# The third low half of the sums ahead of the second unit's slab, in a float32 encoder layer

## The chip, the cores and the metric

The kernel runs on one core of one Trainium2 chip. The metric is the time of one execution on the device in microseconds, the median of several runs; less is better. The core has five engines with instruction queues of their own, which run in order: TensorE (PE, matmuls), VectorE (DVE), ScalarE (ACT), GpSimd (POOL) and SyncE (SP), which here only issues DMAs. They are tied together by semaphores.

## The reference

One layer of a streaming encoder over 512 tokens of width 1024, all in float32:

```python
x = x + 0.5 * swiglu(rms_norm(x, ffn1_norm), ffn1_gate, ffn1_up, ffn1_down)
x = x + hybrid_mixer(rms_norm(x, mix_norm), ...)
x = x + 0.5 * swiglu(rms_norm(x, ffn2_norm), ffn2_gate, ffn2_up, ffn2_down)
return rms_norm(x, final_norm)

def swiglu(h, w_gate, w_up, w_down):
    return (jax.nn.silu(h @ w_gate) * (h @ w_up)) @ w_down
```

The hidden width of a feed-forward is 2816, which is 22 tiles of 128. The mixer (gated linear attention, differential attention and a short convolution) isn't touched here.

## The kernel before

Every float32 product is made as three matmuls of rounded operands: an operand a is split into a high half (a copy to float32r, made by ScalarE) and a low half (a minus its high half, made by VectorE), and `three` (lines 570 to 574) multiplies high by high, high by low and low by high. So each slab of weights, once loaded into `raw`, passes through ScalarE's `split_hi` (line 1118, tile `w_hi`) and VectorE's `split_lo` (line 1496, tile `w_lo`) before TensorE can use it. A slab is 128 partitions by 1024 elements.

A feed-forward has 22 hidden tiles. The first four (`pair`) multiply a gate slab and an up slab in the plain way. The other 18 are **units** of a Strassen-like scheme with seven half-size products in place of eight. A unit v loads a gate slab into `raw` and an up slab into `raw_u`, both double-buffered by v modulo 2. GpSimd (`sums`, lines 483 to 503) makes four sums of their halves:

- T1 = a half of the gate slab plus a half of the up slab (line 491). It waits for both loads, and for VectorE to have read the T1 of the unit before (`ga_lo`).
- T3 = the two halves of the up slab (line 495); T2 = T1 plus the other half of the up slab (line 498); T4 = T2 plus the other half of the gate slab, written over the first half of `raw_u` (line 502). T4 waits for the gate slab's low half (`lo_ready`).

GpSimd makes them in the order T1, T3, T2, T4. ScalarE makes three high halves of them and VectorE three low halves: `ga` (T1 and T2, lines 1198 and 1558), `gb` (T3, lines 1205 and 1563) and `gc` (T4 with the other half of `raw_u`, lines 1237 and 1568).

TensorE's seven products of a unit are M1 and M2 (from the gate slab), M6 and M5 (from ga), M7 (from gb), M4 and M3 (from gc). Its order over units is M1 M2 of unit v, M4 M3 of unit v-1, M6 M5 M7 of unit v; for unit 0 there is no M4 M3 in between. Three products of a unit add up in the same PSUM bank, and ScalarE copies its intermediate states out (`take`, line 1213, tile `snap`): after M1, after M6 and after M7. VectorE combines them: `c11` (lines 1616 and 1619), `c12` (1588), `c21` (1582), `c22` (1576), and `gated` (1596) multiplies with the SiLU that ScalarE makes (1219).

The order of the engines is written out by hand. In VectorE's `unit(v)`: c22 of the unit before, ga, gb, the split of the next unit's slab, c21 of the unit before, c11, c12 of the unit before, gc, gated of the unit before. In ScalarE's: the snapshot of M7 of the unit before, gb, the high half of the next slab, the snapshot of M1, SiLU of the unit before, gc, the snapshot of M6, and ga of the next unit. For unit 0, which has no unit before it, ga and gb are made in the last `pair`, and VectorE's `unit` has only the split of unit 1's slab, c11 and gc.

SyncE's loads (`load_unit`, line 388 on) come in one queue: for unit v the gate slab once T4 of unit v-2 is done (line 396), then the up slab once `gc_lo` of unit v-2 has been counted (line 401). In the first feed-forward alone, a bias table for the mixer is made between units 1 and 2: two matmuls on TensorE (line 590) and two operations on VectorE that follow `gated` of unit 0.

Of the kernel before, what the change touches and what calls it, by code (L numbers as in the profile page):

```python
# [176 lines left out]
def build_layer(nc, xT, up_w, down_w, t_w, dv_w, nat_w, out_w, gains, gk_up, gk_bias, gla_gain, diff_gain,  # L177
                lam_qk, rel_bias, conv_w, onehot, decay_mats, level_masks, ident_c, out):
    tvec = nc.dram_tensor("bias_by_distance", (HEADS * COPIES, 5 * P), F32, kind="Internal")
    with ExitStack() as ctx:  # L180
# [1296 lines left out]
        def _(dve):  # L1477
# [8 lines left out]
            def split_lo(s, n=0):  # L1486

                if isinstance(s, int) and s >= END:
                    return
                dve.wait_ge(hi_ready, n + (s + 1))  # L1490
                w = slab_width(s)
                lo, hi = w_lo[:, slot(s), 0:w], w_hi[:, slot(s), 0:w]
                if isinstance(s, int) and isinstance(n, int) and s >= END - 3:
                    k = KT * (s - (END - 3))
                    lo, hi = (t[:, k:k + w // P, :].rearrange("p k c -> p (k c)") for t in (last_lo, last_hi))
                dve.tensor_tensor(lo, raw[:, slot(s), 0:w], hi, ALU.subtract).then_inc(lo_ready, 1)  # L1496
# [26 lines left out]
            def ffn_up(f, up0):  # L1523
# [32 lines left out]
                def ga(i, b):  # L1556
                    dve.wait_ge(ga_hi, 2 * i + b + (FAST * f + 1))
                    dve.tensor_tensor(sum_lo[:, GA, :], t_raw[:, GA, :], sum_hi[:, GA, :], ALU.subtract)\
                        .then_inc(ga_lo, 1)

                def gb(i, b):
                    dve.wait_ge(gb_hi, 2 * i + b + (FAST * f + 1))
                    dve.tensor_tensor(sum_lo[:, GB, :], t_raw[:, GB, :], sum_hi[:, GB, :], ALU.subtract)\
                        .then_inc(gb_lo, 1)

                def gc(i, b):
                    dve.wait_ge(gc_hi, 2 * i + b + (FAST * f + 1))
                    dve.tensor_tensor(sum_lo[:, GC, :], raw_u[:, b, :].rearrange("p (a c) -> p a c", a=2),
                                      sum_hi[:, GC, :], ALU.subtract).then_inc(gc_lo, 1)

                def c22(i, b):

                    v = 2 * i + b
                    dve.wait_ge(snap_ready[2], v + (FAST * f + 1))
                    dve.wait_ge(m5_done, v + (FAST * f + 1))
                    dve.scalar_tensor_tensor(h[:, PLAIN + v, HALF:S], ps[:, B_BANK[b], 0:HALF], -1.0, snap[:, 2, :],
                                             ALU.mult, ALU.subtract).then_inc(c22_done, 1)

                def c21(i, b):
                    v = 2 * i + b  # L1580
                    dve.wait_ge(m4_done, v + (FAST * f + 1))
                    dve.tensor_tensor(gate_s[:, b, HALF:S], ps[:, A_BANK[b], 0:HALF], rinv[:, HALF:S], ALU.mult)\  # L1582
                        .then_inc(c21_scaled, 1)

                def c12(i, b):
                    v = 2 * i + b
                    dve.wait_ge(m3_done, v + (FAST * f + 1))
                    dve.scalar_tensor_tensor(h[:, PLAIN + v, 0:HALF], ps[:, B_BANK[b], 0:HALF], -1.0, snap[:, 1, :],
                                             ALU.mult, ALU.subtract).then_inc(c12_done, 1)

                def gated(i, b):
                    v = 2 * i + b
                    dve.wait_ge(c12_done, v + (FAST * f + 1))
                    dve.wait_ge(c22_done, v + (FAST * f + 1))
                    dve.wait_ge(silu_done, v + (FT * f + PLAIN + 1))
                    dve.tensor_tensor(h[:, PLAIN + v, :], h[:, PLAIN + v, :], gate_s[:, b, :], ALU.mult)\
                        .then_inc(h_ready, 1)

                def unit(i, b, prev, following):

                    v = 2 * i + b
                    s = up0 + 2 * PLAIN + b
                    if prev:
                        c22(*prev)
                        ga(i, b)
                        gb(i, b)
                    if following:
                        split_lo(s + 1, 2 * i)
                    else:
                        split_lo(s + 2 * i + 1)  # L1610
                    if prev:
                        c21(*prev)
                    dve.wait_ge(h_ready, v + (FT * f + PLAIN - 1))
                    dve.wait_ge(snap_ready[0], v + (FAST * f + 1))
                    dve.wait_ge(slab_used, 2 * i + (s + 1))
                    dve.tensor_tensor(gate_s[:, b, 0:HALF], ps[:, C_BANK[b], 0:HALF], snap[:, 0, :], ALU.add)\
                        .then_inc(c11_added, 1)
                    dve.wait_ge(c11_added, v + (FAST * f + 1))
                    dve.tensor_tensor(gate_s[:, b, 0:HALF], gate_s[:, b, 0:HALF], rinv[:, 0:HALF], ALU.mult)\
                        .then_inc(c11_scaled, 1)  # L1620
                    if prev:
                        c12(*prev)
                    gc(i, b)
                    if prev:
                        gated(*prev)

                for m in range(PLAIN):
                    pair(m)
                unit(0, 0, None, (0, 1))
                unit(0, 1, (0, 0), (1, 0))  # L1630
                if f == 0:
                    bias_table()
                with dve.Fori(1, FAST // 2 - 1) as i:
                    unit(i, 0, (i - 1, 1), (i, 1))
                    unit(i, 1, (i, 0), (i + 1, 0))
# [536 lines left out]
```

## Time and profile before

| | before |
|---|---|
| median of 3 runs | 953.16 us (952.85 to 953.86) |
| profiled execution | 953.2 us, span 951.4 us |
| TensorE matmul busy | 941.7 us (99%) |
| VectorE busy | 685.9 us (72%) |
| ScalarE busy | 435.9 us (46%) |
| GpSimd busy | 358.2 us (38%) |
| granted TensorE clock | 1.00 |

The span runs from the first to the last instruction of the core; the time of the execution holds a little more. Busy is the time in which an engine had an instruction running; one that stands still inside an instruction counts as busy.

### The profile page before, as it was taken

How to read it: one execution, taken by the hardware profiler on the slowest of the kernel's cores; microseconds unless marked ns; L12 is line 12 of the kernel's file. 1: busy time of each engine (PE TensorE's matmuls, PEld its weight loads, DVE VectorE, ACT ScalarE, POOL GpSimd, SP SyncE). 2: the span in 40 equal slices, each digit the busy share in tenths (PEclk: the TensorE clock that was granted, in tenths of full speed). 3: DMA queues.
4: the chain of work that ended last, by engine and by line, in shares of the span. 5: the costliest groups of instructions: out<-in, count | busy, mean ns of one | idle time of the engine just before them, and what ended most of it. 6: DMA issues, size and time to landing. Idle time of an engine off the chain costs nothing.

```text
span 951.4 us, 16549 instructions
## 1 busy us (share of the span) xinstructions
PE 941.7 (99%) x6290; PEld 843.0 (89%) x6290; DVE 685.9 (72%) x956; ACT 435.9 (46%) x686; POOL 358.2 (38%) x241
## 2 busy tenths in 40 slices
PE   9999999999999999999999999999999999999997
PEld 7899999999888889777899788889999999988887
DVE  6699999998543375677578964379999999833444
ACT  7565454556522233654534323544555555632331
POOL 0777777762010135110100015387767676000001
PEclk9999999999999999999999999999999999999999
DMA  6323333232222325222212123233242322232322
GB/s 211 117 105 109 112 95 125 88 131 71 90 100 100 104 79 170 75 74 78 72 57 68 46 88 106 71 133 112 89 132 88 125 96 98 80 100 77 102 99 89
DMA packets 31104, 94.27 MB, mean 99 GB/s; under 512 B 4464, under 2 KB 7712, under 8 KB 31056
## 3 DMA queue, kind: packets, MB, share of 16 engines
q1 hardware_dynamic: 29120, 90.28, 28.8%
q0 software_dynamic: 1648, 3.07, 1.3%
q8 instruction: 33, 0.54, 0.2%
q10 hardware_dynamic: 288, 0.26, 0.1%
q14 instruction: 15, 0.12, 0.0%
HBM read 90.38 MB, written 2.42 MB: 98 GB/s over the span
## 4 chain that ended last, share of the span: by engine, by line
PE 86%; DVE 6%; POOL 2%; ACT 2%; issue 1%; DMA 1%; SPq 0%; DVEq 0%; ACTq 0%; POOLq 0%
PE ps L572 27%; PE ps L574 26%; PE ps L573 26%; POOL h L516 2%; DVE w_lo L1496 1%; DVE s_lo L1553 1%; PE ps L851 1%; PE ps L931 1%; PE ps L872 1%; PE ps L904 1%; ACT h L1126 1%; DVE states L1883 1%; ACT w_hi L1118 1%; DMA x<-xT 0%; PE ps L861 0%
## 5 line engine op out<-in xcount | busy, mean ns | idle before, releaser
L1496 DVE TENSOR_TENSOR w_lo<-raw,w_hi 128x1024 fp32r<-128x1024 f32 (+2 forms) x128 | 195.9, 1530 | 146.0 <-ACT w_hi L1118 146.0
L1118 ACT ACTIVATE w_hi<-raw 128x1024 fp32r<-128x1024 f32 (+2 forms) x128 | 131.3, 1026 | 193.1 <-PE ps L574 193.1
L572 PE MATMUL ps<-xg_hi,w_hi 128*128 128x256 f32 (+1 forms) x528 | 178.2, 338 | 0.8 <-DVE w_lo L1496 0.6
L574 PE MATMUL ps<-xg_hi,w_lo 128*128 128x256 f32 (+1 forms) x528 | 175.0, 331 | 0.0
L573 PE MATMUL ps<-xg_lo,w_hi 128*128 128x256 f32 (+1 forms) x528 | 174.8, 331 | 0.0
L572 PE MATMUL ps<-s_hi,sum_hi 128*128 128x256 f32 x576 | 160.1, 278 | 1.2 <-ACT snap L1213 0.9
L573 PE MATMUL ps<-s_lo,sum_hi 128*128 128x256 f32 x576 | 159.4, 277 | 0.0
L574 PE MATMUL ps<-s_hi,sum_lo 128*128 128x256 f32 x576 | 159.2, 276 | 0.0
L573 PE MATMUL ps<-h_lo,w_hi 128*128 128x512 f32 x330 | 128.4, 389 | 0.0
L572 PEld LDWEIGHTS ps<-xg_hi,w_hi 128*128 128x128 f32 x528 | 99.9, 189 | 19.1 <-issue 8.2
L572 PEld LDWEIGHTS ps<-s_hi,sum_hi 128*128 128x128 f32 x576 | 108.3, 188 | 2.0 <-issue 1.7
L574 PEld LDWEIGHTS ps<-xg_hi,w_lo 128*128 128x128 f32 x528 | 99.9, 189 | 9.9
L573 PEld LDWEIGHTS ps<-s_lo,sum_hi 128*128 128x128 f32 x576 | 108.3, 188 | 0.0
L574 PEld LDWEIGHTS ps<-s_hi,sum_lo 128*128 128x128 f32 x576 | 108.2, 188 | 0.0
L573 PEld LDWEIGHTS ps<-xg_lo,w_hi 128*128 128x128 f32 x528 | 99.9, 189 | 8.5
L574 PE MATMUL ps<-h_hi_s,w_lo 128*128 128x512 f32 x240 | 93.4, 389 | 0.0
L572 PE MATMUL ps<-h_hi_s,w_hi 128*128 128x512 f32 x240 | 93.4, 389 | 0.0
L491 POOL TENSOR_TENSOR t_raw<-raw,raw_u 128x512 f32<-128x512 f32 x36 | 54.9, 1526 | 79.5 <-DMA raw_u<-up_w 68.5
L495 POOL TENSOR_TENSOR t_raw<-raw_u 128x512 f32<-128x512 f32 x36 | 79.6, 2212 | 0.0
L502 POOL TENSOR_TENSOR raw_u<-t_raw,raw 128x512 f32<-128x512 f32 x36 | 71.9, 1998 | 11.5 <-POOL t_raw L498 7.0
L573 PEld LDWEIGHTS ps<-h_lo,w_hi 128*128 128x128 f32 x330 | 62.0, 188 | 12.6
L1219 ACT ACTIVATE gate_s<-gate_s 128x512 f32<-128x512 f32 x34 | 21.5, 634 | 110.5 <-DVE gate_s L1582 110.5
(255 smaller groups left out, 1891.5 us busy)
## 6 DMA issues: line engine op xcount, KB each, us to landing
raw<-up_w SPq DMA_DIRECT2D x50, 512.0 KB, 4.1
raw<-down_w SPq DMA_DIRECT2D x38, 512.0 KB, 3.2
raw_u<-up_w SPq DMA_DIRECT2D x36, 512.0 KB, 3.2
raw<-t_w SPq DMA_DIRECT2D x15, 512.0 KB, 3.2
raw<-out_w SPq DMA_DIRECT2D x8, 512.0 KB, 3.2
raw<-nat_w SPq DMA_DIRECT2D x4, 576.0 KB, 3.8
x<-xT SPq DMA_DIRECT2D x8, 256.0 KB, 4.8
out<-x SPq DMA_DIRECT2D x8, 256.0 KB, 2.2
```

The costliest lines, as they stand in the source:

```text
L491: pool.tensor_tensor(t_raw[:, T1, :], raw[:, slot(s), 0:HW], raw_u[:, b, 0:HW], ALU.add)\
L495: pool.tensor_tensor(t_raw[:, T3, :], raw_u[:, b, 0:HW], raw_u[:, b, HW:UPW], ALU.add)\
L502: pool.tensor_tensor(raw_u[:, b, 0:HW], t_raw[:, T2, :], raw[:, slot(s), HW:UPW], ALU.add)\
L516: pool.tensor_tensor(out_ap, in0, in1, op).then_inc(s_made, 1)
L572: pe.matmul(out_ap, a[0], b[0], start=first, stop=False, skip_group_check=resumed)
L573: pe.matmul(out_ap, a[0], b[1], start=False, stop=False, skip_group_check=resumed)
L574: return pe.matmul(out_ap, a[1], b[0], start=False, stop=last, skip_group_check=resumed)
L851: last = pe.matmul(ps[:, 4 + mp, 0:w], dqk[r, h % 2, 0, i * P:(i + 1) * P], dqk[r, h % 2, 1, 0:w], start=True, stop=True)
L872: last = pe.matmul(ps[:, 7, 0:DV], pT[:, n % 2, b * P:(b + 1) * P], dv[:, b, h * DV:(h + 1) * DV], start=b == 0, stop=b == i)
L1118: act.activation(dst, raw[:, slot(s), 0:w], ACT.Copy).then_inc(hi_ready, 1)
L1219: act.activation(gate_s[:, b, :], gate_s[:, b, :], ACT.Silu).then_inc(silu_done, 1)
L1496: dve.tensor_tensor(lo, raw[:, slot(s), 0:w], hi, ALU.subtract).then_inc(lo_ready, 1)
```

## The change

In `unit` of VectorE's feed-forward, for the first unit (the one without a `prev`), `gc` is issued ahead of `split_lo` of the next unit's slab; before, it was issued last, behind c11. All other units keep their order. The code is used by both feed-forwards, so two places of the run are touched.

```diff
@@ -1604,6 +1604,8 @@
                         c22(*prev)
                         ga(i, b)
                         gb(i, b)
+                    else:
+                        gc(i, b)
                     if following:
                         split_lo(s + 1, 2 * i)
                     else:
@@ -1620,8 +1622,7 @@
                         .then_inc(c11_scaled, 1)
                     if prev:
                         c12(*prev)
-                    gc(i, b)
-                    if prev:
+                        gc(i, b)
                         gated(*prev)
```

## Rows read from the trace of the kernel before

**Rows 1.** The page: busy us, share of the span and instructions of each engine.

```profile
PE 941.7 (99%) x6290; PEld 843.0 (89%) x6290; DVE 685.9 (72%) x956; ACT 435.9 (46%) x686; POOL 358.2 (38%) x241
```

**Rows 2.** Timeline of TensorE, second feed-forward: start us, length us, instruction, idle before and releaser.

```profile
648.99 0.28 PE L572 MATMUL ps<-xg_hi,w_hi 128*128 128x256 f32 x1
...
657.62 0.36 PE L572 MATMUL ps<-s_hi,sum_hi 128*128 128x256 f32 x1
...
667.36 0.28 PE L574 MATMUL ps<-s_hi,sum_lo 128*128 128x256 f32 x1
668.50 0.36 PE L572 MATMUL ps<-s_hi,sum_hi 128*128 128x256 f32 x1 [0.86 <-ACT snap L1213]
```

**Rows 3.** Chain that ended last, from 640 to 672 us: start us, us, what.

```profile
651.39 3.20 DMA raw_u<-up_w
```

**Rows 4.** Timeline of VectorE, second feed-forward, units 0 to 2.

```profile
642.39 2.33 DVE L1558 TENSOR_TENSOR sum_lo<-t_raw,sum_hi 128x1024 fp32r<-128x1024 f32 x1
...
645.84 1.72 DVE L1496 TENSOR_TENSOR w_lo<-raw,w_hi 128x1024 fp32r<-128x1024 f32 x1
...
648.91 2.31 DVE L1568 TENSOR_TENSOR sum_lo<-raw_u,sum_hi 128x1024 fp32r<-128x1024 f32 x1
651.54 0.42 DVE L1576 SCALAR_TENSOR_TENSOR h<-ps,snap 128x256 f32<-128x256 f32 x1 [0.32 <-ACT snap L1213]
651.88 1.58 DVE L1558 TENSOR_TENSOR sum_lo<-t_raw,sum_hi 128x1024 fp32r<-128x1024 f32 x1
...
653.98 1.21 DVE L1496 TENSOR_TENSOR w_lo<-raw,w_hi 128x1024 fp32r<-128x1024 f32 x1
...
658.79 1.78 DVE L1596 TENSOR_TENSOR h<-h,gate_s 128x512 f32<-128x512 f32 x1
661.55 0.42 DVE L1576 SCALAR_TENSOR_TENSOR h<-ps,snap 128x256 f32 x1 [0.99 <-ACT snap L1213]
...
663.77 2.31 DVE L1496 TENSOR_TENSOR w_lo<-raw,w_hi 128x1024 fp32r<-128x1024 f32 x1
```

**Rows 5.** Timeline of GpSimd, second feed-forward, units 1 to 3.

```profile
644.89 1.59 POOL L491 TENSOR_TENSOR t_raw<-raw,raw_u 128x512 f32<-128x512 f32 x1 [1.25 <-DVE sum_lo L1558]
646.43 2.27 POOL L495 TENSOR_TENSOR t_raw<-raw_u 128x512 f32<-128x512 f32 x1
648.66 1.48 POOL L498 TENSOR_TENSOR t_raw<-t_raw,raw_u 128x512 f32<-128x512 f32 x1
...
654.75 1.60 POOL L491 TENSOR_TENSOR t_raw<-raw,raw_u 128x512 f32<-128x512 f32 x1 [2.38 <-DMA raw_u<-up_w]
...
663.42 1.57 POOL L491 TENSOR_TENSOR t_raw<-raw,raw_u 128x512 f32<-128x512 f32 x1 [1.70 <-DVE sum_lo L1558]
```

**Rows 6.** Timeline of ScalarE, second feed-forward: three snapshots.

```profile
651.15 0.36 ACT L1213 ACTIVATE snap<-ps 128x256 f32<-128x256 f32 x1
...
657.12 0.36 ACT L1213 ACTIVATE snap<-ps 128x256 f32<-128x256 f32 x1
...
667.99 0.36 ACT L1213 ACTIVATE snap<-ps 128x256 f32<-128x256 f32 x1
```

**Rows 7.** Timeline of VectorE, first feed-forward: the splits for units 1 and 2.

```profile
58.76 1.71 DVE L1496 TENSOR_TENSOR w_lo<-raw,w_hi 128x1024 fp32r<-128x1024 f32 x1
...
66.91 1.21 DVE L1496 TENSOR_TENSOR w_lo<-raw,w_hi 128x1024 fp32r<-128x1024 f32 x1
```

**Rows 8.** Timeline of GpSimd, first feed-forward: T1 and T2 of unit 1.

```profile
57.81 1.59 POOL L491 TENSOR_TENSOR t_raw<-raw,raw_u 128x512 f32<-128x512 f32 x1 [1.25 <-DVE sum_lo L1558]
...
61.59 1.48 POOL L498 TENSOR_TENSOR t_raw<-t_raw,raw_u 128x512 f32<-128x512 f32 x1
```

**Rows 9.** Timeline of ScalarE, first feed-forward: the snapshot of M6 of unit 1.

```profile
70.03 0.36 ACT L1213 ACTIVATE snap<-ps 128x256 f32<-128x256 f32 x1
```

**Rows 10.** Timeline of TensorE, first feed-forward: M1 and M7 of unit 1.

```profile
62.05 0.28 PE L572 MATMUL ps<-xg_hi,w_hi 128*128 128x256 f32 x1
...
70.54 0.36 PE L572 MATMUL ps<-s_hi,sum_hi 128*128 128x256 f32 x1
```

## The prediction

> **What bounds the kernel.** I read the page first: TensorE is busy 941.7 us of a span of 951.4 [rows 1]. It sets the time nearly everywhere, so an edit on VectorE counts only where TensorE waits. The second view is TensorE's timeline in the first units of a feed-forward [rows 2]. Below, M1 to M7 are a unit's seven products. TensorE makes M1 and M2 of a unit from its slab, then M4 and M3 of the unit before, then M6, M5 and M7 of the unit itself. T1 to T4 are GpSimd's four additions, in the order T1, T3, T2, T4. "Ga", "gb" and "gc" are VectorE's three low halves of the sums. Units count from 0.
>
> In the second feed-forward the reader is to see that matmuls follow each other by about 0.11 us, but from 667.36 to 668.50 there are 1.14 us: M7 of unit 2 starts 1.03 us late, released by ScalarE's snapshot. The third view, the chain of waits, leads from there back to the load of unit 2's up slab, which begins at 651.39 [rows 3]. That load waits for gc of unit 0, which ends at 651.22 (648.91 + 2.31) [rows 4]. GpSimd's T1 of unit 2 starts at 654.75, 3.53 us after the end of that gc, although VectorE's ga of unit 1, its other condition, ended at 653.46 [rows 4, 5]. So there is a stall of about 1 us that hangs on gc. In the first feed-forward TensorE reaches the same place without such a gap, because the two matmuls of the bias table stand between units 1 and 2.
>
> **How VectorE and GpSimd interleave.** The change exchanges two instructions of equal shape, so their lengths matter less than what they meet. The split takes 1.21 us at 653.98, 1.72 at 645.84 and 2.31 at 663.77 [rows 4]. The long ones always overlap a GpSimd addition, and their ends fit one rule: a VectorE subtraction of 1024 elements that started while GpSimd was inside an addition ends 1.08 us after that addition (646.48 to 647.56; 664.99 to 666.08), and a GpSimd addition that started while VectorE was inside such an instruction ends 1.15 us after it (647.56 to 648.70; 655.19 to 656.35) [rows 4, 5]. One of the two stands still while the other runs. gc of unit 0 does the same: T2 ends at 650.14, gc at 651.22.
>
> The Trainium skill, page "SBUF — State Buffer", section "SBUF: two separate sides", says that the port pair common to VectorE and GpSimd is an exclusive lock held for a whole instruction, and not a split of bandwidth. By a split of bandwidth the exchange would cost next to nothing (rival A); by a lock it changes who stands behind whom. The trace's constant 1.08 and 1.15 us speak for the lock.
>
> **What the change adds, step by step, second feed-forward.** No instruction is added or removed, and no DMA. Only gc of unit 0 goes ahead of the split of unit 1's slab. Its input is there: ScalarE's high half of it precedes its next snapshot by far, and VectorE was only free at 645.84.
> 1. gc starts at 645.84 inside T1 of unit 1 (ends 646.48) and ends at 647.56, where the split ended. It was 651.22: gc is 3.66 us earlier. T3 still ends at 648.70 [rows 4, 5].
> 2. The split now starts at 647.48, inside T3, and ends at 648.70 + 1.08 = 649.78. It was 647.56. TensorE started M1 of unit 1 at 648.99 without a stop [rows 2]. A split's result reaches TensorE about 0.15 us after its end (an estimate from the snapshot that ends at 657.48 and the matmul at 657.62 [rows 2, 6]), so M1 starts at 649.93: **0.94 us of new stall**. Nothing hides it; the cover of the old order, 1.43 us, is gone.
> 3. T2 of unit 1 started at 648.66 and ended at 650.14 because VectorE had only small operations from PSUM then. Now it stands behind the split: 649.78 + 1.15 = 650.93, 0.79 us later. ScalarE's high half of ga waits for T2, and its snapshot of M7 (651.15 + 0.36 = 651.51) is queued behind that: it ends at 652.30. VectorE waits for this snapshot for c22 of unit 0: 651.54 becomes 652.33 [rows 4 to 6]. TensorE's M4, later by 0.94 itself, doesn't wait for it.
> 4. ga of unit 1 follows at 652.67. It no longer meets T4 (0.12 behind T2, some 1.5 us long as T2 was: until 652.5) and takes 1.21, not 1.58: it ends at 653.88 (was 653.46). The second low half follows, 0.60 us further.
> 5. Here comes what the earlier load triggers. Unit 2's up slab is asked for about 647.7 and in place by 651.1. T1 of unit 2 therefore no longer waits for it, only for ga. In unit 1, where it also waited for ga alone, T1 ended 1.76 us after ga's end (642.39 + 2.33 = 644.72 to 646.48) [rows 4, 5], so now it runs to 653.88 + 1.76 = 655.64. In the trace of before it came late enough to fall behind the split of unit 2's slab. Now it starts (654.05) ahead of that split (654.40), which ends at 655.64 + 1.08 = 656.72 in place of 655.19: **1.53 us later**.
> 6. c21 of unit 0 follows the split, ScalarE's SiLU waits for c21, and behind SiLU in ScalarE's queue stand the third high half and the snapshot of M6: 657.48 becomes 659.01 [rows 6]. M7 of unit 1 waits for it: 659.15 in place of 657.62. TensorE's own lag of 0.94 would have had it at about 658.3, so TensorE stops once more, and its lag is now 1.53.
> 7. The relief. The product gated of unit 0 ended at 660.57 (658.79 + 1.78) and VectorE then sat idle for 0.99 until c22 of unit 1 [rows 4]. The 1.53 of lag use that up: gated ends at 662.10, c22 starts at 662.02 (was 661.55) and ga ends as far behind it as in step 4 (652.33 to 653.88): 663.57. Unit 3's up slab is asked for 1.53 later than before; its T1 starts 3.53 after gc's end of 660.40, at 663.93 (was 663.42). It meets the second low half, ends 1.76 after ga's end at 665.33 (was 664.99), the split of unit 3 at 666.41 (was 666.08), the snapshot at 668.68 (was 668.35) [rows 4 to 6].
> 8. M7 of unit 2 could start, without a stop, at 667.36 + 0.11 + 1.53 = 669.00; the snapshot allows 668.82. The stall of 1.03 us is gone, and a restart after a stop (0.08 us more than a running matmul's pitch: 0.19 against 0.11) goes with it. Lag behind it: 1.53 - 1.03 - 0.08 = **0.42 us**. Behind this VectorE is 0.33 and TensorE 0.42 us late. TensorE had no gap in the following units, and has none then.
>
> **First feed-forward.** The same steps with its rows: T1 of unit 1 ends at 59.40, gc at 60.48, T3 at 61.63, the split at 62.71; TensorE wanted it at 62.05, and gets it at 62.86: 0.81 us [rows 7 to 10]. T2 goes from 63.07 to 63.86, +0.79 as above; from T2's end to the end of the split of unit 2 steps 3 to 5 take 656.72 - 650.93 = 5.79, so it ends at 69.65 in place of 68.12. The snapshot of M6 (70.39) and M7 of unit 1 (70.54) are late by the same: **1.53 us**, 0.81 of it already in M1. No stall stands behind it that could be given back: the bias matmuls start and end 1.5 later, VectorE's bias table follows them directly as before, and unit 2 begins with the same relations between the engines.
>
> **Sum.** 1.53 + 0.42 = 1.95 us. What comes between and behind is TensorE-bound or a chain that starts from what TensorE has done, so I give nothing back. The profiled execution took 953.2 us (span 951.4, 1.8 around it), practically the median of 953.16. Forecast: 953.16 + 1.95 = 955.1 us.
>
> Ends of the unknown terms: a split in second place lasts between 1.21 us (its shortest row, no stall at all: nothing lost, the whole 1.03 gained) and the 2.31 of the longest row. I take 2.31, since the rule gives it and the overlap with T3 is certain. The collision of step 5 costs between 0 and 1.1 us per feed-forward; I take all of it, with only 0.35 us of margin in who starts first.
>
> **Rivals.**
> A, a small gain: the instructions share instead of excluding each other, and the order matters as little as their equal shapes suggest. The split in second place lasts 1.72, as in first. TensorE gets it at 649.35 and 62.26: 0.36 and 0.21 lost, the first partly swallowed by the stop of about 0.23 that M7 of unit 1 had anyway; the 1.0 comes back. -1.0 + 0.13 + 0.21 = -0.7: 952.5 us. It decides if the split ends before 648.8 and 61.9. For it: the change takes away exactly the wait that the chain shows. Against it: 1.08 and 1.15 in every pair.
> B, the collision of step 5 doesn't happen, since T1 of unit 2 starts after the split. Then the vector chain is late by only 0.42. First feed-forward 0.81; second: 0.7 after M7 of unit 1, then M7 of unit 2 stops as before, less long, and 0.4 remains. 953.2 + 1.2 = 954.4 us.
> C, step 7 doesn't give back: the margin of 0.18 us between snapshot and M7 of unit 2 is lost when unit 3's load lands later or a lag is met by another collision. Then 1.0 to 1.1 us more, 956.2 us.
> That gc would wait for its high half in its new place, so that VectorE stands still in front of the split, the rows exclude: VectorE comes to it about 1 us after that half was made.
>
> **Chances.** Forecast 0.68 (its own range 954.7 to 955.5), A 0.14, B 0.10, C 0.08. A measurement of this kernel tells about 0.2% from no change, 1.9 us; the forecast stands right on that bound, so its 0.68 are halved, 0.34 and 0.34. Slower: 0.34 + 0.08, and 0.02 taken from A for losses not seen, 0.44. Within 0.2%: 0.34 + 0.10 of A + 0.10 of B, 0.54. Faster: the rest of A, 0.02. The range of 953.3 to 956.3 leaves out A and little else.
>
> **What would show it.** In the changed kernel's trace: gc of unit 0 of 1.7 us directly ahead of a split of 2.3 us; a gap of TensorE of 0.7 to 0.9 us ahead of M1 of unit 1 in both feed-forwards, released by that split; a second one ahead of M7 of unit 1, released by a ScalarE snapshot; T1 of unit 2 waiting for ga in place of the DMA; a split of unit 2 of about 2.3 us; no stall at M7 of unit 2 in the second feed-forward. A split of unit 1 that ends within 1.3 us of its start, or a split of unit 2 that still takes 1.2, makes the prediction wrong.

## The result, and the profile after

The changed kernel takes 954.97 us (median of 19 runs, 954.32 to 956.24) against 952.98 us of the kernel before (19 runs, 952.27 to 953.86). The ratio is 1.0021, with a 95% interval of 1.0015 to 1.0027: slower by 1.99 us, where 955.1 us and an increase of 1.95 us had been forecast.

| | before | after |
|---|---|---|
| median | 952.98 us | 954.97 us |
| span of the profiled execution | 951.4 us | 953.5 us |
| TensorE matmul busy | 941.7 us | 941.6 us |
| VectorE busy | 685.9 us | 687.8 us |
| GpSimd busy | 358.2 us | 359.1 us |

TensorE does the same work; of the 2.1 us of span, 1.9 lie in its pauses in the two feed-forwards. Its timeline in the second has two of them. In the kernel before, M1 of unit 1 starts without a stop, and M7 of unit 1 comes 0.35 us after the matmul ahead of it, where 0.11 is the distance without a stop:

```profile
651.68 0.36 PE L572 MATMUL ps<-xg_hi,w_hi 128*128 128x256 f32 x1 [0.78 <-DVE w_lo L1496]
...
660.88 0.36 PE L572 MATMUL ps<-s_hi,sum_hi 128*128 128x256 f32 x1 [0.55 <-ACT snap L1213]
```

The first is M1 of unit 1, released by the split (`w_lo`), the second M7 of unit 1, released by a ScalarE snapshot. At M7 of unit 2, where the kernel before stood still for 0.86 us, the matmuls now run through, 0.12 us from start to start:

```profile
670.61 0.28 PE L574 MATMUL ps<-s_hi,sum_lo 128*128 128x256 f32 x1
670.73 0.28 PE L572 MATMUL ps<-s_hi,sum_hi 128*128 128x256 f32 x1
```

Around M1 and M7 of unit 1 in the first feed-forward:

```profile
63.08 0.35 PE L572 MATMUL ps<-xg_hi,w_hi 128*128 128x256 f32 x1 [0.79 <-DVE w_lo L1496]
...
72.29 0.36 PE L572 MATMUL ps<-s_hi,sum_hi 128*128 128x256 f32 x1 [0.56 <-ACT snap L1213]
```

VectorE in the second feed-forward, against [rows 4]. All stands 1.75 us later here than in the trace of before, by what had been lost until then (M6 of unit 0 starts at 646.57 against 644.82), so 1.75 is to be taken off:

```profile
647.59 1.71 DVE L1568 TENSOR_TENSOR sum_lo<-raw_u,sum_hi 128x1024 fp32r<-128x1024 f32 x1
649.22 2.31 DVE L1496 TENSOR_TENSOR w_lo<-raw,w_hi 128x1024 fp32r<-128x1024 f32 x1
...
651.90 1.06 DVE L1621 TENSOR_TENSOR gate_s<-gate_s,rinv 128x256 f32<-128x256 f32 x1
654.07 0.42 DVE L1576 SCALAR_TENSOR_TENSOR h<-ps,snap 128x256 f32<-128x256 f32 x1 [1.11 <-ACT snap L1213]
654.41 1.21 DVE L1558 TENSOR_TENSOR sum_lo<-t_raw,sum_hi 128x1024 fp32r<-128x1024 f32 x1
...
656.15 2.31 DVE L1496 TENSOR_TENSOR w_lo<-raw,w_hi 128x1024 fp32r<-128x1024 f32 x1
...
662.03 1.77 DVE L1596 TENSOR_TENSOR h<-h,gate_s 128x512 f32<-128x512 f32 x1
663.74 0.41 DVE L1576 SCALAR_TENSOR_TENSOR h<-ps,snap 128x256 f32 x1
...
665.80 2.31 DVE L1496 TENSOR_TENSOR w_lo<-raw,w_hi 128x1024 fp32r<-128x1024 f32 x1
```

gc (line 1568) now stands ahead of the split (line 1496) and takes 1.71 us; the split takes 2.31. The split of unit 2, 1.21 us before, is the row at 656.15 with 2.31. GpSimd beside it, against [rows 5]:

```profile
646.63 1.58 POOL L491 TENSOR_TENSOR t_raw<-raw,raw_u 128x512 f32<-128x512 f32 x1 [1.25 <-DVE sum_lo L1558]
648.18 2.27 POOL L495 TENSOR_TENSOR t_raw<-raw_u 128x512 f32<-128x512 f32 x1
650.41 2.26 POOL L498 TENSOR_TENSOR t_raw<-t_raw,raw_u 128x512 f32<-128x512 f32 x1
...
655.70 1.67 POOL L491 TENSOR_TENSOR t_raw<-raw,raw_u 128x512 f32<-128x512 f32 x1 [1.59 <-DVE sum_lo L1558]
...
665.65 1.39 POOL L491 TENSOR_TENSOR t_raw<-raw,raw_u 128x512 f32<-128x512 f32 x1 [2.38 <-DMA raw_u<-up_w]
```

T2 of unit 1 (line 498) lasts 2.26 in place of 1.48 us. T1 of unit 2 at 655.70 no longer waits for the DMA of the up slab but for ga, and it is under way when the split of unit 2 comes at 656.15. ScalarE's snapshots, against [rows 6]:

```profile
653.67 0.36 ACT L1213 ACTIVATE snap<-ps 128x256 f32<-128x256 f32 x1
...
660.37 0.36 ACT L1213 ACTIVATE snap<-ps 128x256 f32<-128x256 f32 x1
...
670.03 0.36 ACT L1213 ACTIVATE snap<-ps 128x256 f32<-128x256 f32 x1
```

VectorE and GpSimd in the first feed-forward, against [rows 7, 8]:

```profile
58.99 1.72 DVE L1568 TENSOR_TENSOR sum_lo<-raw_u,sum_hi 128x1024 fp32r<-128x1024 f32 x1
60.63 2.31 DVE L1496 TENSOR_TENSOR w_lo<-raw,w_hi 128x1024 fp32r<-128x1024 f32 x1
...
67.55 2.31 DVE L1496 TENSOR_TENSOR w_lo<-raw,w_hi 128x1024 fp32r<-128x1024 f32 x1
```

### The profile page after: what moved, and what is told of

The parts are those of the page before. It is cut to its first block, busy times and chain, and to the rows that moved or that the text cites. A ratio compares the mean times of both kernels' runs of the same rounds, so it can differ in the third digit from the quotient of the medians.

```text
span 953.5 us, 16549 instructions
## 1 busy us (share of the span) xinstructions
PE 941.6 (99%) x6290; PEld 842.4 (88%) x6290; DVE 687.8 (72%) x956; ACT 436.8 (46%) x686; POOL 359.1 (38%) x241
## 4 chain that ended last, share of the span: by engine, by line
PE 87%; DVE 7%; POOL 2%; ACT 2%; issue 1%; DMA 1%; SPq 0%; DVEq 0%; POOLq 0%; ACTq 0%
PE ps L572 28%; PE ps L574 27%; PE ps L573 27%; POOL h L516 2%; DVE w_lo L1496 1%; DVE s_lo L1553 1%; PE ps L851 1%; PE ps L931 1%; PE ps L872 1%; PE ps L904 1%; ACT h L1126 1%; DVE states L1884 1%; ACT w_hi L1118 1%; DMA x<-xT 1%; DVE sum_lo L1558 0%
## 5 line engine op out<-in xcount | busy, mean ns | idle before, releaser
L1496 DVE TENSOR_TENSOR w_lo<-raw,w_hi 128x1024 fp32r<-128x1024 f32 (+2 forms) x128 | 198.2, 1549 | 146.2 <-ACT w_hi L1118 146.1
```

## The experiments

All were run on one core against the kernel before on the same chip. The times differ by little, so the verdict is read mostly from the trace. The distances come from one profiled execution of each kernel. The measure is how long after M6 of unit 0 TensorE starts M1 of units 1, 2 and 3 (start of the first `ps<-xg_hi,w_hi` matmul of each); what is lost ahead of that place doesn't enter. The two executions with the old order in a feed-forward (before and e1, before and e2) agree in it within 0.05 us at units 2 and 3. At unit 1 it is 4.17 or 4.31 us in kernels that do the same there (see the last section).

| kernel | 1st: M1 of units 1, 2, 3 | 2nd: M1 of units 1, 2, 3 | median, us | before beside it |
|---|---|---|---|---|
| before | 4.31, 15.62, 25.49 | 4.17, 14.25, 25.13 | | |
| after | 5.11, 17.17, 27.03 | 5.11, 15.75, 25.52 | 954.97 | 952.98 |
| e1, first only | 5.12, 17.13, 27.00 | 4.32, 14.30, 25.15 | 954.48 | 953.23 |
| e2, second only | 4.18, 15.62, 25.49 | 5.11, 15.76, 25.52 | 953.34 | 953.23 |
| e5, split then gc | 4.32, 17.19, 27.06 | 4.31, 15.80, 25.56 | 954.74 | 953.23 |
| e3, load held | 5.11, 16.31, 26.18 | 5.11, 14.95, 25.61 | 954.05 | 953.23 |
| e4, short T3 | 4.17, 16.06, 25.93 | 4.16, 14.68, 24.44 | 952.73 | 953.03 |
| e10, two snapshots | 5.11, 17.13, 26.99 | 5.12, 15.77, 25.53 | 955.05 | 952.87 |
| e6, c21 early | 4.16, 16.04, 26.65 | 4.18, 14.72, 25.57 | 954.92 | 953.03 |
| e8, e6 with two snapshots | 4.17, 15.29, 25.16 | 4.17, 13.93, 24.12 | 954.60 | 953.09 |
| e7, c21 early in all | 4.17, 15.29, 25.16 | 4.32, 14.09, 24.29 | 957.38 | 953.09 |
| e9, c21 early once | 4.17, 15.29, 25.42 | 4.31, 14.26, 25.14 | 952.88 | 952.87 |

### e1 and e2: one feed-forward at a time

```diff
-                    else:
+                    elif f == 0:        # e2: f == 1
                         gc(i, b)
...
+                    elif f == 1:        # e2: f == 0
+                        gc(i, b)        # last, as before
```

> The new order in the first feed-forward alone; the second keeps the old one. Theory L (VectorE's and GpSimd's two-input operations exclude each other, and the loss is what the queues make of it): TensorE loses 1.5 us here, in two gaps, about 0.8 us ahead of M1 of unit 1 and the rest ahead of M7 of unit 1; the second feed-forward keeps its stop of 0.86 us at M7 of unit 2. About +1.5 us against before, 954.5. Rival R (the loss is only how late the split of unit 1's slab is): +0.8 us, 953.8.

> The new order in the second feed-forward alone. Theory L: +0.4 us against before (1.5 lost in two gaps, 1.1 given back at M7 of unit 2), 953.4: not told from no change by the times, but M1 of unit 3 stands 0.39 us later in the trace, counted from M6 of unit 0. Rival R: 0.94 lost and 1.03 given back, -0.1 us.

Measured: at unit 3 the first feed-forward alone costs 27.00 - 25.49 = 1.51 us, the second alone 25.52 - 25.13 = 0.39. The ratios are 1.0015 (1.0006 to 1.0024) and 1.0002 (0.9993 to 1.0011). Together they are the 1.5 + 0.4 of the changed kernel, so the places don't act on each other, and the rival's 0.8 for the first is out. The second is nearly free only because a stop of 1.0 us disappears beside the new ones.

### e5: the split first, then gc, then c11

```diff
                     if prev:
                         c21(*prev)
+                    else:
+                        gc(i, b)
```

> Both feed-forwards; unit 0 makes split, gc, c11 in this order, so the split of unit 1's slab is in time as before, and gc is still ahead of c11. Theory L: no gap ahead of M1 of unit 1. gc now meets T3 and lasts 2.3 us, T2 stands behind it and ends as late as in the changed kernel (0.79 us late), so the snapshot that M4 of unit 0 needs is late: a gap of some 0.6 us ahead of M4. The up slab of unit 2 is still early enough (1.4 us earlier than before) for T1 of unit 2 to go ahead of the split of unit 2's slab, and M7 of unit 1 comes as late as in the changed kernel. The sum is that of the changed kernel: +1.9 us, 954.9. Rival R: the split is in time, so nothing is lost and the stop at M7 of unit 2 goes: -1.0 us, 952.0.

TensorE in the second feed-forward of e5:

```profile
653.61 0.35 PE L572 MATMUL ps<-xg_hi,sum_hi 128*128 128x256 f32 x1 [0.29 <-ACT snap L1213]
...
660.31 0.36 PE L572 MATMUL ps<-s_hi,sum_hi 128*128 128x256 f32 x1 [0.93 <-ACT snap L1213]
```

GpSimd's T2 of unit 1 there:

```profile
649.81 2.29 POOL L498 TENSOR_TENSOR t_raw<-t_raw,raw_u 128x512 f32<-128x512 f32 x1
```

M1 of unit 1 is in time (4.31), as the split is. The pause sits at M4 instead (0.29 idle, 0.58 from start to start against 0.12), and M7 of unit 1 comes 14.34 us after M6 of unit 0 (660.31 - 645.97), as in the changed kernel (660.88 - 646.57 = 14.31). At unit 3 the sum is 1.57 + 0.43 = 2.0 us, that of the changed kernel. The time is 1.0017 (1.0008 to 1.0026) of before. So the loss doesn't need a late split. With gc in second place T2 is late by the same 0.8 us, and the split of unit 2's slab is held up as in the changed kernel (2.31 us). What both orders share is a second long instruction of VectorE ahead of T2, and an earlier load of unit 2's up slab; e3 tells these two apart.

### e3: the up slab's load held back

```diff
                     sp.wait_ge(gc_lo, v + (FAST * f - 1))
+                    sp.wait_ge(c11_scaled, v + (FAST * f - 1))
                 sp.dma_start(raw_u[:, b, :], up_w[f, v + PLAIN, 1]).then_inc(u_loaded[b], 16)
```

> The changed kernel, but SyncE also waits for the scaled c11 of unit v-2 before it loads the up slab of unit v, which puts the load of unit 2's up slab back to where it was before the change. Theory L: the gap of 0.8 to 0.9 us at M1 of unit 1 stays; T1 of unit 2 starts 0.3 us after the split of unit 2's slab, which takes 1.2 us and not 2.3; no gap at M7 of unit 1. In the second feed-forward the stop at M7 of unit 2 returns, at some 0.4 us. First feed-forward +0.8, second +0.1: +0.9 us against before, 953.9, 1.0 us less than the changed kernel. Rival P (the earlier load is a help, and holding it back can only cost): later than the changed kernel by up to 1.0 us, the stop at M7 of unit 2.

VectorE's split and GpSimd's T1 of unit 2 in the second feed-forward of e3 (its line numbers are one higher):

```profile
654.66 1.22 DVE L1497 TENSOR_TENSOR w_lo<-raw,w_hi 128x1024 fp32r<-128x1024 f32 x1
```

```profile
655.01 2.03 POOL L492 TENSOR_TENSOR t_raw<-raw,raw_u 128x512 f32<-128x512 f32 x1 [2.38 <-DMA raw_u<-up_w]
```

```profile
669.20 0.36 PE L573 MATMUL ps<-s_hi,sum_hi 128*128 128x256 f32 x1 [0.60 <-ACT snap L1214]
```

With the load at its old time T1 comes 0.35 us after the split, and the split takes 1.22 us again. There is no pause at M7 of unit 1 in either feed-forward. At M7 of unit 2 in the second the stop returns with 0.60 us. Against before at unit 3: 0.69 + 0.48 = 1.17 us, and 0.76 less than the changed kernel. The time is 1.0011 (1.0002 to 1.002) of before. Holding a load back took 0.76 us out of the changed kernel's loss, so rival P is out. The 0.13 expected for the second feed-forward was 0.48: T1 stands behind the split in both kernels, and that split itself ends 0.43 us later than before, by the late T2 and c22 of step 3. T1 then ends 0.43 us later too (11.96 against 11.53 after M6 of unit 0), and ScalarE and c22 pass that on in full; I had given the chain to the snapshot less than that. By the prediction's rival B this state was priced at 1.2 us.

### e4: T3 of unit 1 cut to 8 columns

```diff
+                n3 = 8 if isinstance(i, int) and v == 1 else HW
-                pool.tensor_tensor(t_raw[:, T3, :], raw_u[:, b, 0:HW], raw_u[:, b, HW:UPW], ALU.add)
+                pool.tensor_tensor(t_raw[:, T3, 0:n3], raw_u[:, b, 0:n3], raw_u[:, b, HW:HW + n3], ALU.add)
```

> The changed kernel, with GpSimd's T3 of unit 1 cut from 512 to 8 columns in both feed-forwards (the rest of that sum is left out, so the unit's result is not the reference's). Theory L: the split of unit 1's slab stands behind T3 only. With T3 short it takes about 1.2 us in second place, no gap ahead of M1 of unit 1; T2 stands behind the split but ends 0.2 us earlier than in the kernel before. T1 of unit 2 still goes ahead of the split of unit 2's slab, so a gap of 0.5 to 0.7 us ahead of M7 of unit 1 stays. The stop at M7 of unit 2 in the second feed-forward is gone. First +0.5, second -0.6: about -0.1 us against before, 2.0 less than the changed kernel. Rival S (a subtraction right behind another of the same shape is slow by itself, whatever GpSimd does): the split stays at 2.3 us and the gap at M1 at 0.8.

The other 504 columns of that sum are left out, so this kernel is a question put to the trace and nothing to keep. VectorE's gc of unit 0 and split of unit 1, and GpSimd's T3 and T2, in its second feed-forward:

```profile
645.99 1.72 DVE L1569 TENSOR_TENSOR sum_lo<-raw_u,sum_hi 128x1024 fp32r<-128x1024 f32 x1
647.63 1.22 DVE L1497 TENSOR_TENSOR w_lo<-raw,w_hi 128x1024 fp32r<-128x1024 f32 x1
```

```profile
646.58 1.19 POOL L496 TENSOR_TENSOR t_raw<-raw_u 128x8 f32<-128x8 f32 x1
647.73 2.28 POOL L499 TENSOR_TENSOR t_raw<-t_raw,raw_u 128x512 f32<-128x512 f32 x1
```

The split right behind gc now takes 1.22 us, and TensorE has no pause at M1 of unit 1 (4.16 us). It has the one at M7 of unit 1 (0.51 us). T2 took 2.28 us behind the split. At unit 3: +0.44 and -0.69, sum -0.25 against before; the time is 0.9998 (0.9989 to 1.0007) of it. So the split in second place is long because of GpSimd's T3, and rival S is out.

### e10: the changed kernel with two buffers for the snapshot of M6

```diff
+        def snap1(b):
+            return conv_cb[:, 0:HALF] if b else snap[:, 1, :]
...
-                        act.wait_ge(used, v + FAST * f)
+                        act.wait_ge(used, v + FAST * f - (1 if two else 0))
```

> The changed kernel with two buffers for the snapshot of M6 and nothing else. It asks which of two waits makes the second gap, ahead of M7 of unit 1: ScalarE's queue (SiLU, which waits for c21) or the buffer (c12 of unit 0). In the changed kernel's trace both end within 0.1 us of each other, so theory Q: freeing the buffer alone changes nothing, both gaps and the time stay, 954.9. Rival: the buffer is the wait, the second gap shrinks by 0.3 us or more in each feed-forward, 954.3.

The distances are those of the changed kernel within 0.04 us, and the ratio is 1.0022 (1.0013 to 1.0031). So in the changed kernel ScalarE's queue is enough for the second pause, as the prediction has it, and freeing the buffer alone changes nothing.

### e6 and e8: c21 ahead of gb in units 1 and 2

```diff
                         ga(i, b)
+                        if early:          # units 1 and 2, both feed-forwards
+                            c21(*prev)
                         gb(i, b)
```

e8 is e6 with the two buffers of e10.

> The kernel before, with c21 of the unit before made ahead of gb, and so ahead of the split, in units 1 and 2 of each feed-forward alone (the third and fourth unit of the loop stand outside it for that). It follows from theory L: M7 of units 1 and 2 waits for a ScalarE snapshot, which is queued behind SiLU, which waits for c21, which stands behind the split that GpSimd holds up. With c21 ahead of the split the snapshots are in time. Second feed-forward: the stops at M7 of unit 1 (0.3 us with its restart) and of unit 2 (1.1 us) both go, -1.4 us; first: -0.1 us. 951.7 against 953.2, faster than both kernels. Against it (rival R): VectorE waits for M4 in front of c21 and passes that on to ga and the splits of later units, which stop TensorE again: no gain.

> The kernel of the previous question (c21 ahead of gb in units 1 and 2 of each feed-forward), in which ScalarE's snapshot of M6 now has two buffers, by unit modulo 2, so that it needn't wait until VectorE has read the one of the unit before (c12). Theory T: in that kernel the snapshot waited for c12, which stands behind the split just as c21 did. With two buffers the stops at M7 of units 1 and 2 go in both feed-forwards. But VectorE's chain isn't faster by it, and where its old order returns, in unit 3 of the second feed-forward, TensorE stops for 1.0 to 1.7 us at M7: second feed-forward about 0, first -0.1; 953.0. Rival U: only SiLU and c21 matter, the buffer changes nothing, and the time stays at 954.9.

e6 was a miss: 954.92 us, 1.0020 (1.0011 to 1.0029) of before, where 951.7 was expected. ScalarE in its second feed-forward shows why:

```profile
655.37 0.64 ACT L1219 ACTIVATE gate_s<-gate_s 128x512 f32<-128x512 f32 x1 [0.78 <-DVE gate_s L1582]
656.23 1.07 ACT L1237 ACTIVATE sum_hi<-raw_u 128x1024 fp32r<-128x1024 f32 x1 [0.23 <-PE ps L574]
658.88 0.38 ACT L1213 ACTIVATE snap<-ps 128x256 f32<-128x256 f32 x1 [1.58 <-DVE h L1588]
```

SiLU and the third high half are early, but the snapshot of M6 then waits 1.58 us for `h` of line 1588, which is c12 of unit 0: it is to overwrite the snapshot that c12 reads, and c12 too stands behind the split. In the kernel before c12 ends at 656.96 and the snapshot starts at 657.12 straight behind ScalarE's work before it, so the two waits end almost together, and I had seen the one only.

With two buffers (e8) the pauses at M7 of units 1 and 2 are gone in both feed-forwards (a new one of 0.21 us stands at M4 of unit 1 in the second): unit 3 starts 0.33 and 1.01 us earlier than in the kernel before. But one unit later TensorE stops again at M7, by 0.44 us in the first feed-forward and by 1.18 in the second (a snapshot each, written to `conv_cb`):

```profile
92.19 0.36 PE L575 MATMUL ps<-s_hi,sum_hi 128*128 128x256 f32 x1 [0.44 <-ACT conv_cb L1217]
```

```profile
679.64 0.36 PE L575 MATMUL ps<-s_hi,sum_hi 128*128 128x256 f32 x1 [1.18 <-ACT conv_cb L1217]
```

M1 of unit 4 is then 0.38 and 0.46 us later than before (35.63 against 35.25, 35.35 against 34.89). The time was 954.60 us, 1.0014 (1.0005 to 1.0023) of before, where 953.0 was expected, so theory T had the place of the stops and not their sum. About 0.3 us of the loss arises between the feed-forwards (0.4 in e6), and I haven't found where. I read the stops as the places where TensorE waits for a chain of VectorE and GpSimd that is about as long as its own; these two runs fit that, and e7 gives the chain's pace.

### e7: c21 ahead of gb in every unit

> The kernel before, with c21 of the unit before ahead of gb in every unit but the last step, and two buffers for the snapshot of M6. Theory T: TensorE no longer waits for a snapshot behind VectorE's split in any unit; no gap at M7 of units 1 and 2. VectorE's chain, at some 9.7 us a unit against TensorE's 9.76, can sustain it. -1.4 us in the second feed-forward, -0.1 in the first: 951.6. Against it: in the first feed-forward, where VectorE is ahead of TensorE, it now idles until M4 is made, 1 to 2 us in every unit, and if the rest of its unit doesn't fit in what is left, TensorE stops in every unit, up to 0.5 us each and 15 us in all.

This too was a miss: 957.38 us, 1.0047 (1.0034 to 1.0061) of before, where 951.6 was expected. No pause at M7 is left in any early unit. Until unit 8 of the first feed-forward M1 is 0.3 us ahead of before; from there on a unit takes 9.8 to 10.2 us where the kernel before takes 9.76, and M1 of unit 17 is 1.97 us behind (164.10 against 162.13 after M6 of unit 0). In the second feed-forward the same begins at unit 6, and M1 of unit 17 is 1.94 us behind (163.71 against 161.77). The mean is 10.0 us a unit in both, against the 9.7 that the expectation gave VectorE's chain.

The idle column shows next to nothing of it. A matmul is drawn with 0.28 us while the next starts 0.11 us later, so a stop of up to 0.17 us is no idle time; TensorE's busy time rose instead, from 941.7 to 946.9 us. The stops are seen from start to start, between M4's last matmul and M3's first, which waits for c22. In unit 9 of the first feed-forward it is 0.28 us where it is 0.12 without a stop:

```profile
145.62 0.28 PE L577 MATMUL ps<-xg_hi,sum_lo 128*128 128x256 f32 x1
145.90 0.39 PE L575 MATMUL ps<-s_hi,sum_hi 128*128 128x256 f32 x1
```

Units 13 and 16 have the same there (0.27 and 0.26 us); in the second feed-forward ten of the units 6 to 16 have 0.20 to 0.29. In the first, about half of the loss lies behind that place: in six of the units 9 to 16 the matmuls of M3, M6, M5 and M7 follow each other by 0.118 us in place of 0.114, which makes 0.19 us a unit (see the last section). In the second only unit 6 has that, and its units take the same 10.0 us. So I read the 10.0 as the pace of the chain that TensorE waits for, and not as the price of the slower matmuls; no run here separates the two. The expectation named the stops as its risk, at up to 15 us in all.

### e9: c21 early in unit 1 of the first feed-forward alone

> The kernel before, with c21 of unit 0 ahead of gb in unit 1 of the first feed-forward alone, and two buffers for the snapshot of M6. It takes the one gain that stayed in the early units of the two kernels tried before: M1 of unit 2 stood 0.33 us earlier there, counted from M6 of unit 0. Theory T: in this feed-forward the bias matmuls leave VectorE enough room to keep its chain in time, so the 0.33 stay in every later unit; 952.7 against 953.1, seen in the trace and not in the times. Rival: the next units pay it back (as unit 3 did in the kernel with two early units), 953.1.

Unit 2 starts 0.33 us earlier, unit 3 only 0.07 (25.42 against 25.49). The rival was right. The ratio is 1.000 (0.9991 to 1.0009). None of the versions that compute the whole result beats the kernel before.

## Why the prediction was right

The forecast was 955.1 us and the measured 954.97, an increase of 1.95 against 1.99, in steps that the trace of after confirms one by one. Second feed-forward, with 1.75 us taken off:

| step | forecast | measured |
|---|---|---|
| 1. gc of unit 0 ends | 647.56 | 647.55 |
| 2. split of unit 1 ends; M1 starts | 649.78; 649.93 | 649.78; 649.93 |
| 3. T2 of unit 1 ends; c22 of unit 0 starts | 650.93; 652.33 | 650.92; 652.32 |
| 4. ga of unit 1 ends | 653.88 | 653.87 |
| 5. T1 and the split of unit 2 end | 655.64; 656.72 | 655.62; 656.71 |
| 6. snapshot of M6 ends; M7 of unit 1 | 659.01; 659.15 | 658.98; 659.13 |
| 7. gated of unit 0 ends; T1 of unit 3 starts | 662.10; 663.93 | 662.05; 663.90 |
| 8. M7 of unit 2 starts; lag behind it | 669.00; 0.42 | 668.98; 0.39 |

**Steps 1 and 2** rest on the turns of VectorE and GpSimd, with 1.08 and 1.15 us behind each other's end. e4 shows that T3 is what the split stands behind: without a long T3 it takes 1.22 and the pause is gone. That alone would fit a sharing as well; what decides against rival A is the length beside a long T3, 2.31 where it had 1.72.

**Step 3** has one reading wrong that its sum didn't need. It says that T2 of unit 1 ran beside "only small operations from PSUM" of VectorE in the kernel before. The second half of c11 (line 1619) has both operands in SBUF, and T2 stood behind it:

```profile
647.93 1.06 DVE L1619 TENSOR_TENSOR gate_s<-gate_s,rinv 128x256 f32<-128x256 f32 x1
```

It ends at 648.99, and T2 at 650.14, 1.15 us later: the prediction's own rule, and the reason why T2 took 1.48 us there and not the 1.3 that an addition takes with nothing ahead of it. The new end of T2 was worked out from the split, so the forecast didn't suffer.

**Steps 3 to 6**: e5 shows that T2 and what follows carry the loss even where the split is in time. e3 shows the collision in step 5: with the load late again, the same code loses 0.76 us less. e10 shows that in this kernel ScalarE's queue makes the snapshot late even where its buffer is free. Rival B needed T1 of unit 2 to start behind the split. In the trace it starts 0.45 us ahead of it; the forecast had given that race 0.35 us.

**Steps 7 and 8**: e2 isolates 0.39 us. The stop at M7 of unit 2 is gone, and rival C's further loss didn't come.

**First feed-forward**: forecast 1.53, measured 1.54 at unit 3 (1.51 in e1). From M6 of unit 0 in the first to M6 of unit 0 in the second feed-forward the changed kernel takes 588.60 us and the one before 587.08: the 1.52 passed through the whole mixer and nothing was given back, as the sum assumed.

What wasn't in the forecast: of the 2.1 us of span, 0.2 come from the start of the kernel, where M6 of unit 0 starts at 57.97 against 57.74. Other runs show 57.35 to 58.19 there without a change in that part, so that is the spread of the stretch ahead of it. The prediction took 0.2% for the smallest change that can be told from none. Its forecast lay so near to it that it gave "slower" a chance of 0.44 only: it was surer of the mechanism than of what the times alone would tell.

## What to carry to other kernels

Ahead of exchanging two equal instructions of VectorE, look at what GpSimd has in hand at either moment, and write down both engines' starts and ends, which pass the turn to each other. Ask of a transfer that comes earlier which work it sets off earlier, and in front of what that work then stands: here a load that was 3.7 us earlier cost 0.8 us. Where TensorE's stop came from another engine's chain, putting that chain in another order moved the stop to a later unit in e8, e7 and e9. Work taken out of the chain was a gain that stayed: with the same order, e4 stands 1.1 us ahead of the changed kernel in either feed-forward, at unit 3 and at unit 4.

## What the runs showed of the hardware

VectorE's operations that read two operands from SBUF and GpSimd's additions took turns in all kernels here: for 1024 elements 1.21 us alone and up to 2.31 when the other was inside an instruction, and 1.22 again when GpSimd had only 8 columns to add. In the trace of before 79 such subtractions took over 1.3 us, and 74 of them end 1.07 to 1.10 us behind the end of a GpSimd instruction. A sharing by proportion wouldn't give one constant. VectorE's operations with one operand in PSUM stayed at 0.41 us beside the same additions. The Trainium skill, page "SBUF — State Buffer", section "Who interferes with whom", says that a VectorE instruction with two inputs in SBUF contends with a GpSimd instruction that reads SBUF, that one with at most one SBUF input, outside the modes that use both ports, doesn't, and that the order of issue and not the shape decides who blocks. The rows agree on all three: e3 and the changed kernel run the same split in 1.22 and in 2.31 us, by 0.35 us of lead or 0.45 us of lag.

TensorE's cadence has two values for the same matmuls: the 36 matmuls from M6 to M7 of unit 0 took 4.17 us in some executions and 4.31 in others, at a granted clock of 1.00, and the kernel before had 4.31 in its first and 4.17 in its second feed-forward, e7 the reverse. In the twelve traces together there are 430 stretches of 30 or more of these matmuls of sums without a stop inside. All 386 that ran on from the matmul ahead have 0.114 us from start to start; of the 44 that started behind a stop, 15 have 0.118, over their whole length. What decides between the two behind a stop, I don't know. At units 2 and 3 it changed nothing in these kernels, where M7 of unit 1 waits for a snapshot anyway.
